# A first norm on half of its features, four projection units side by side, and a decay table that is loaded later

## The reference

```python
mod = c @ ada_w[l] + ada_b[l]
sh1, sc1, gt1, sh2, sc2, gt2 = [m[:, None, :] for m in jnp.split(mod, 6, axis=-1)]
h = rmsnorm(x, norm1_g[l]) * (1.0 + sc1) + sh1
p = h @ w_in[l]
xr, yr, q, k, v, ga, gb = jnp.split(p, cuts, axis=-1)
```

## Time and profile before

| | us |
|---|---|
| median of 3 runs | 1707.73 (1707.16 to 1708.38) |
| the profiled execution | 1710.79 |
| its span | 1709.0 |
| PE busy in it | 1653.0 |
| span until PE's first projection product | 42.56 |
| mean granted TensorE clock | 0.988 |

### The profile page before, as it was taken

One profiled execution on the slowest core, in us unless ns is written; L12 is line 12 of the kernel. 1 busy time (PEld: TensorE's weight loads), 2 busy tenths in 40 slices (PEclk: granted clock), 3 DMA queues, 4 the chain that ended last, 5 costly groups with the idle time before them and its releaser, 6 DMA issues.

```text
span 1709.0 us, 19726 instructions
## 1 busy us (share of the span) xinstructions
PE 1653.0 (97%) x7340; PEld 1345.3 (79%) x7340; DVE 982.8 (58%) x1170; ACT 801.3 (47%) x1005; POOL 785.1 (46%) x577
## 2 busy tenths in 40 slices
PE   3999999999989999999999999999999999999997
PEld 2778787877768888888887888777878888888885
DVE  6676788777637817715643767566436554155541
ACT  2565565666434425414442233676653544244442
POOL 1244443444455545554563544455573252543425
PEclk7999999999989999999999999999999999999999
DMA  9333333232222232232322322211222131321312
GB/s 367 123 123 124 123 111 124 94 128 87 85 94 98 95 101 89 99 123 99 99 86 68 111 95 71 72 42 56 75 86 76 50 109 50 99 99 50 99 50 74
DMA packets 46463, 166.89 MB, mean 98 GB/s; under 512 B 5153, under 2 KB 5281, under 8 KB 45857
## 3 DMA queue, kind: packets, MB, share of 16 engines
q1 hardware_dynamic: 46368, 165.63, 28.7%
HBM read 163.52 MB, written 2.10 MB: 97 GB/s over the span
## 4 chain that ended last, share of the span: by engine, by line
PE 89%; DVE 4%; POOL 3%; issue 1%; ACT 1%; DMA 1%; SPq 0%; POOLq 0%; DVEq 0%; ACTq 0%
PE lin L651 16%; PE lin L653 16%; PE lin L652 16%; PE big L651 7%; PE big L653 7%; PE big L652 7%; DVE scr L1580 1%; POOL sq_sum L595 1%; PE big L757 1%; PE m_o L777 1%; PE big L768 1%; PE big L770 1%; PE big L1065 1%; PE big L1063 1%; PE big L1064 1%
## 5 line engine op out<-in xcount | busy, mean ns | idle before, releaser
L617 POOL TENSOR_TENSOR w_lo<-raw,w_hi 128x512 fp32r<-128x512 f32 x200 | 283.1, 1415 | 647.4 <-ACT w_hi L1100 647.4
L651 PE MATMUL lin<-h_hi,w_hi 128*128 128x512 f32 x936 | 368.3, 394 | 4.5 <-POOL w_lo L620 1.8
L653 PE MATMUL lin<-h_hi,w_lo 128*128 128x512 f32 x936 | 364.6, 390 | 0.0
L652 PE MATMUL lin<-h_lo,w_hi 128*128 128x512 f32 x936 | 364.4, 389 | 0.0
L620 POOL TENSOR_TENSOR w_lo<-raw,w_hi 128x512 fp32r<-128x512 f32 x209 | 301.5, 1443 | 14.4 <-ACT w_hi L1100 14.4
L1100 ACT ACTIVATE w_hi<-raw 128x1024 fp32r<-128x1024 f32 (+1 forms) x209 | 217.6, 1041 | 159.8 <-PE m_b L669 50.3
L651 PEld LDWEIGHTS lin<-h_hi,w_hi 128*128 128x128 f32 x936 | 175.8, 188 | 42.4 <-issue 3.4
L653 PEld LDWEIGHTS lin<-h_hi,w_lo 128*128 128x128 f32 x936 | 175.7, 188 | 37.1
L652 PEld LDWEIGHTS lin<-h_lo,w_hi 128*128 128x128 f32 x936 | 175.9, 188 | 36.3 <-issue 0.7
L617 POOL TENSOR_TENSOR qk_hl<-raw,qk_hl 128x512 fp32r<-128x512 f32 x43 | 59.6, 1387 | 159.0 <-ACT qk_hl L1100 159.0
L651 PE MATMUL lin<-y_hi,w_hi 128*128 128x512 f32 x260 | 101.6, 391 | 0.0
(11 more groups left out here) (493 smaller groups left out, 3435.9 us busy)
## 6 DMA issues: line engine op xcount, KB each, us to landing
raw<-weights SPq DMA_DIRECT2D x245, 512.0 KB, 3.5
slab<-ada SPq DMA_DIRECT2D x32, 512.0 KB, 4.1
scr<-ada SPq DMA_DIRECT2D x16, 512.0 KB, 6.3
raw<-weights SPq DMA_DIRECT2D x10, 256.0 KB, 2.6
x<-x_t SPq DMA_DIRECT2D x2, 1024.0 KB, 6.0
out_t<-scr SPq DMA_DIRECT2D x8, 256.0 KB, 2.6
raw<-weights SPq DMA_DIRECT2D x4, 448.0 KB, 3.3
rgw<-rg_w SPq DMA_DIRECT2D x1, 1024.0 KB, 7.1
```

What stands on the lines that cost most here:

```text
L617: nc.gpsimd.tensor_tensor(lo[:, 0:4 * P], raw[:, s, 0:4 * P], hi[:, 0:4 * P].bitcast(F32), ALU.subtract).then_inc(w_half, 1)
L651: nc.tensor.matmul(psum_of(n), wh, hi(k), start=(k == 0), stop=False)
L652: nc.tensor.matmul(psum_of(n), wh, lo(k), start=False, stop=False)
L653: last = nc.tensor.matmul(psum_of(n), wl, hi(k), start=False, stop=(k == nk - 1))
```

## The change

- The slabs of the first modulation are laid out anew: slabs 0 to 7 now hold shift and scale of features 0 to 511, slabs 8 to 15 those of the other half. After 8 slabs PE forms 8 sums, and DVE, after the first 10 slabs, norms tiles 0 to 3; then come slabs 10 to 15, the second sum, tiles 4 to 7.
- The root goes to the PSUM bank `m_a` instead of `rstd`, and the scaled x of the first norm to `big[:, 2]` and `m_b` in turn instead of the four tiles `tmp`.
- PE works off tiles 0 to 3 of q0 and k0, then tiles 0 to 3 of v0 and q1, the second modulation sum, then tiles 4 to 7 of both pairs. v0 and q1 get the PSUM banks `big[:, 0]` and `big[:, 1]`; before the scores of head 0, PE waits for `v_copied` 1 and `q_copied` 2.
- A third window of two homes (in rows 2 to 5 of `y_hi` and `y_lo`) is open from q0 to v1. The homes are now q0 0, k0 1, v0 2, q1 7, k1 8, v1 0 (behind q0), xr0 1 (behind k0), yr0 2 (behind v0), ga0 0 (behind v1). Before they were q1 0 (behind q0), k1 1 (behind k0), v1 2 (behind v0), xr0 0 (behind q1), yr0 1 (behind k1), ga0 2 (behind v1).
- SP's ring: slabs 0 to 9, q0, k0, 10, 11, v0, 12 to 15, q1, 16, k1, 17, v1, 18, 19, rgw, the decay table, xr0, 20, 21, yr0, ga0, 22.
- ACT splits q0, k0, v0, then does h_hi for tiles 0 to 3, splits q1, and does tiles 4 to 7.

```diff
+NEARLY = CONST["diff"][0]
...
-            units += [("q", 0, 8), ("k", 0, 8), ("v", 0, 8), ("ada", a, 8), ("ada", a + 1, 8), ("q", 1, 8),
-                      ("ada", a + 2, 8), ("k", 1, 8), ("ada", a + 3, 8), ("v", 1, 8), ("ada", a + 4, 8)]
+            units += [("ada", i, 8) for i in range(10)] + [("q", 0, 8), ("k", 0, 8), ("ada", 10, 8), ("ada", 11, 8)]
+            units += [("v", 0, 8)] + [("ada", i, 8) for i in range(12, ADA_FIRST)]
+            units += [("q", 1, 8), ("ada", a, 8), ("k", 1, 8), ("ada", a + 1, 8), ("v", 1, 8), ("ada", a + 2, 8),
+                      ("ada", a + 3, 8)]
...
+        if h == 1:
+            units += [("ada", a, 8)]
...
-    windows = ((("w_out", 3), ("p_out", 6), None), (("a_out", 0), ("rv", 2), ("qn", HEADS - 1)))
+    windows = ((("w_out", 3), ("p_out", 6), None), (("a_out", 0), ("rv", 2), ("qn", HEADS - 1)),
+               (("q", 0), ("v", 1), None))
...
+        if (kind, j) in (("v", 0), ("q", 1)):
+            bank[n] = 2 if kind == "v" else 3
...
+        def scaled(r, k):
+            if r == 0:
+                return (big[:, 2], m_b[:])[k % 2]
+            return tmp[:, k % 4]
...
-            sp.dma_start(cst[:], consts).then_inc(cst_loaded, 16)
+            sp.dma_start(cst[:, 0:NEARLY], consts[:, 0:NEARLY]).then_inc(cst_loaded, 16)
...
                     sp.dma_start(rgw[:], rg_w).then_inc(rgw_loaded, 16)
+                    sp.dma_start(cst[:, NEARLY:NCONST], consts[:, NEARLY:NCONST]).then_inc(diff_loaded, 16)
...
-                    pair(("q", 0), ("k", 0), H, L, normed(0))
-                elif h < HEADS:
+                    for part in (range(4), range(4, DK)):
+                        if part[0]:
+                            modulation(1)
+                        pair(("q", 0), ("k", 0), H, L, normed(0), part)
+                        pair(("v", 0), ("q", 1), H, L, normed(0), part)
+                elif 1 < h < HEADS:
                     unit("q", h, H, L)
                 if h == 1:
                     unit("k", h, H, L)
+                    pe.wait_ge(v_copied, 1)
+                    pe.wait_ge(q_copied, 2)
...
-            norm_root(square_used, 8, D)
-            split_ahead(0)
-            highs(0)
+            norm_root(square_used, 8, D, m_a[:])
+            split_ahead(0, 2)
+            highs(0, range(4))
+            split_ahead(0, 3)
+            highs(0, range(4, DK))
...
-            for a in range(ADA_FIRST):
-                accumulate(a)
-            dve.wait_ge(mod_done, 2)
+            for half in range(2):
+                for a in range(10) if half == 0 else range(10, ADA_FIRST):
+                    accumulate(a)
+                dve.wait_ge(mod_done, half + 1)
...
+                if half == 0:
+                    dve.wait_ge(x_loaded, 32)
+                    dve.wait_ge(norm_rooted, 1)
+                norm_apply(0, lambda k: sm(A1 + k), lambda k: sm(MOD + k), m_a[:], 4 * half, 4 * half + 4)
...
+            dve.wait_ge(diff_loaded, 16)
             for h in range(RH):
...
-    ada = i["ada_w"][0].reshape(DK, P, 6, D).transpose(1, 2, 0, 3).reshape(P, NADA, 2, T)
+    ada = i["ada_w"][0].reshape(DK, P, 6, D).transpose(1, 2, 0, 3).reshape(P, 6, DK, 2, T)
+    ada[:, 0:2] = ada[:, 0:2].transpose(0, 3, 2, 1, 4).copy()
+    ada = ada.reshape(P, NADA, 2, T)
```

More of the change, by code:

```diff
@@ L45 @@
 _at = 0
-for _name, _n in (("ident", P), ("later_ones", 2 * P), ("ones", P), ("mask", P), ("diff", T + 3 * P),
-                  ("freq_a", 1), ("freq_r", 1)):
+for _name, _n in (("ident", P), ("later_ones", 2 * P), ("ones", P), ("mask", P), ("freq_a", 1),
+                  ("freq_r", 1), ("diff", T + 3 * P)):
     CONST[_name] = (_at, _n)
@@ L184, in bank_plan @@
             turn[ring] = 0
-        bank[n] = turn[ring] % ring
-        turn[ring] += 1
+        if (kind, j) in (("v", 0), ("q", 1)):
+            bank[n] = 2 if kind == "v" else 3
+        else:
+            bank[n] = turn[ring] % ring
+            turn[ring] += 1
         before[n] = last.get(bank[n])
@@ L511, in home @@
                 return spare[:, i - HOMES, 0], spare[:, i - HOMES, 1]
-            of = (cq_hi, cq_lo)[i - HOMES - SPARE][:].rearrange("p a t -> p (a t)")
-            return of[:, 0:8 * P], of[:, 8 * P:16 * P]
+            if i < HOMES + 2 * SPARE:
+                of = (cq_hi, cq_lo)[i - HOMES - SPARE][:].rearrange("p a t -> p (a t)")
+                return of[:, 0:8 * P], of[:, 8 * P:16 * P]
+            rows = slice(2 * (i - HOMES - 2 * SPARE) + 2, 2 * (i - HOMES - 2 * SPARE) + 4)
+            return y_hi[:, rows].rearrange("p a t -> p (a t)"), y_lo[:, rows].rearrange("p a t -> p (a t)")
         def weights_of(n):
@@ L562, in _ @@
                     sp.dma_start(inv_count, inv_counts).then_inc(inv_loaded, 16)
+                if kind == "ada" and j < ADA_FIRST:
+                    if j >= 6:
+                        sp.wait_ge(ada_used, j - 5)
+                    sp.dma_start(ada_in[:, j % 6], ada[:, j]).then_inc(ada_loaded[j % 6], 16)
+                    continue
                 if kind == "ada":
@@ L709, in modulation @@
                 for m in range(DK):
[L710 removed]
+                    at = 8 * (m // 4) + 4 * g + m % 4
+                    out = m_o[:, at:at + 1] if g < 2 else m_b[:, 8 * g - 16 + m:8 * g - 15 + m]
                     last = nc.tensor.matmul(out, acc[:, m // 4, (m % 4) * P:(m % 4 + 1) * P], c_("ones")[:, 0:1],
@@ L713, in modulation, with pair @@
                 last.then_inc(mod_done, 1)
-            def pair(a, b, hi, lo, ready):
+            def pair(a, b, hi, lo, ready, part=range(DK)):
                 na, nb = UNIT[a], UNIT[b]
                 for n in (na, nb):
-                    if BEFORE[n] is not None:
+                    if BEFORE[n] is not None and part[0] == 0:
                         pe.wait_ge(*freed(n))
-                for k in range(DK):
+                for k in part:
                     pe.wait_ge(*ready(k))
@@ L1170, in gate, with highs @@
                 act.wait_ge(rgate_done, counted(rgate_done))
-            def highs(r):
-                for k in range(DK):
+            def highs(r, part=range(DK)):
+                for k in part:
                     act.wait_ge(pre_h, DK * r + k + 1)
-                    nc.scalar.activation(h_hi[:, k], tmp[:, k % 4], ACT.Identity,
+                    nc.scalar.activation(h_hi[:, k], scaled(r, k), ACT.Identity,
                                          bias=sm(MOD + 24 * r + k)).then_inc(h_high, 1)
@@ L1595, in _, with norm_apply @@
             dve.wait_ge(dve_order, counted(dve_order))
[L1596 to L1601, removed]
+            def norm_apply(r, gain, shift, factor, first=0, last=DK):
+                for k in range(first, last + 1):
+                    if k < last:
+                        v.scalar_tensor_tensor(out=scaled(r, k), in0=x[:, k], scalar=gain(k), in1=factor,
                                                op0=M, op1=M).then_inc(pre_h, 1)
                         dve.wait_ge(pre_h, counted(pre_h))
-                    if k > 0:
+                    if k > first:
                         e = k - 1
                         dve.wait_ge(h_high, DK * r + e + 1)
-                        v.scalar_tensor_tensor(out=h_lo[:, e], in0=tmp[:, e % 4], scalar=shift(e),
+                        v.scalar_tensor_tensor(out=h_lo[:, e], in0=scaled(r, e), scalar=shift(e),
                                                in1=h_hi[:, e].bitcast(F32), op0=AD, op1=SU).then_inc(h_low, 1)
```

36 lines of the change are left out of this document (16 added, 20 removed).

## The result

The changed kernel takes 1724.72 us, the median of 4 runs (1722.45 to 1726.07), against 1707.76 for the kernel before (1707.16 to 1708.38) beside it: a ratio of 1.0094, with a 95% interval of 1.0082 to 1.0107. It is slower by 17.0 us, and the forecast was 12.8. The profiled execution took 1726.07 us with a span of 1724.0, 15.0 us more than the span of before.

What follows compares the result with a forecast made beforehand. PE, with work for 97% of the span, bounds the kernel; head 0 ends 14.7 us later, 1.9 comes back, so 1707.7 + 12.8 = 1720.5 us, range 1714 to 1725.

Steps and rivals of the forecast that it cites:

- The start: First half norm and projections: PE's first product at 31.5 us instead of 42.56, second sum ending 47.2, restart 50.4.
- The clock in the second half: PE after the second modulation sum: lower clock, q0 and k0 done at 58.5; if held, 2.2 us less, 1718.3.
- The first wait: ACT must split late-loaded xr0 before copying v0: copy at 76.8 instead of 63.16, PE idle 12 us before the transposes.
- The second wait: ACT must split yr0, landing at 87.6, before copying q1: head 0's scores at 89.3 instead of 74.62.
- only the first wait: Rival: yr0 lands before PE is through k1 (85.6), 3.7 us less, 1716.8; chance 0.05.
- The scores' clock: Variant: clock fallen also before head 0's scores, which run at half pace, 2 us more, 1722.6.
- What comes back: Between scores and suffix sums, xr0 and yr0 being split already: 1.9 us regained (1.4 to 2.4).
- The sum: Whole kernel: +14.7 for head 0's later end, -1.9 back, so +12.8 us: 1720.5.
- The mechanism: In at(), ACT splits every weight whose home is free before each copy, so copies stand behind late xr0 and yr0.
- The faster rival: No wait binds, xr0 and yr0 there in time: scores at 71.0, 5.5 us gained, 1702.2; chance 0.08.

Runs made afterwards that it cites:

- e1: Changed kernel, but ahead of copying v0 ACT splits no unit beyond v1; xr0 and yr0 are split ahead of q1's copy: 1714.82 us, ratio 1.0035.
- e2: Changed kernel, but ahead of copying v0 and q1 ACT splits nothing beyond v1; xr0 and yr0 are split ahead of k1's copy: 1706.16 us, ratio 0.9987.
- e3: Changed kernel with only SP's order altered: xr0 and yr0 loaded ahead of slab 19, gate weights and decay table ahead of slab 20: 1704.61 us, ratio 0.9980.
- e4_loads_early_busy: e3 plus 13 PE products with zeros into q0's bank, between the second modulation sum and the second half: 1708.42 us, ratio 0.9995.
- e7_busy_logs_first: e4_loads_early_busy with DVE's chain of 23 small steps (logs of decays) moved ahead of its wait for the constants: 1703.34 us, ratio 0.9973.

## Why the prediction was right, and where it was off

- **The start.** First product forecast 31.5, measured 32.07; second sum 45.3 to 47.2, measured 46.00 to 47.95; restart 50.4, measured 50.90: 0.5 to 0.8 us late throughout. Two steps inside were off without showing. The first sum took 3.15 us, not the 1.95 of before, so DVE had its first product at 27.48 instead of 25.3, but ACT was not through with v0's split before 30.45. And DVE's six accumulations took 9.70 us, not 7.9 to 8.9, so they ended at 45.75, beside PE's products and not ahead of them: the second sum waited for DVE (0.17 us), where the forecast had PE as the later one. The price of the norm's operands in PSUM, bounded at 0.75 and 1.7, was 0.76, beside POOL too.
- **The clock in the second half** was taken as low, and the window 50 to 52 has 0.50. The products of q0 and k0 were done at 59.27 against 58.5, when v0's began.
- **The first wait.** Slab 16 accumulated at 66.15 for 65.0, SP on at 66.2 for 65.1: 0.7 of this is k0's late square (63.81 for 63.1), and 0.3 the step that makes its low part, 1.45 us beside POOL (63.91) instead of 1.11. xr0 landed 8.6 us behind slab 19 (74.84), where I had 9.9 from the rows of before: the gate weights took 5.8 from issue to landing, not 7.1. The two errors cancel, 74.8 against 75.0. By the Trainium skill (DMA: Bandwidth & Descriptors, Anatomy of one DMA), whose fit is of transfers issued from GpSimd and not from SP, it was 7.9, an estimate; the measured 8.6 lies between, a little nearer to the page. v0 copied at 76.5 for 76.8; 10.42 us of idle time for 12.
- **The second wait.** Slab 18 accumulated at 82.68, forecast 82.7. yr0 landed 5.1 us after its issue, not 4.5: 88.18 for 87.6, and so the scores at 89.97 for 89.3. k1 was done at 84.6 for 85.6, so PE idled 5.32 us there and not 3.7. That yr0 landed behind k1's end also rules out the rival "only the first wait".
- **The scores' clock: the term that was mis-sized.** The forecast ran the scores at full pace, and put the lower clock before them down as a variant, 1722.6. That variant came: 4.58 us for 2.32. At k1's end the clock had been at 2.4 GHz; PE then idled 5.32 us, and the window 88 to 92 has 0.50.
- **What comes back** was put at 1.9. From the scores to the suffix sums it was 14.55 forecast, 16.40 measured; before it was 16.46. With 2.26 for the scores' clock the rest is 14.1, in the forecast's own range (14.0 to 15.1). So 2.3 came back, where 1.9 was forecast, and was lost to the clock. It came from DVE's chain, which ends with cq_lo and for which PE still waited 0.42: from its first step it took 7.7 us (98.64 to 106.32) instead of 10.0 (81.03 to 91.02), with fewer of POOL's subtractions beside it.
- **The sum.** In profiled executions +15.3 against +12.8: 0.7 from the scores' late start, 2.3 from their clock, less 0.4 from the chain behind them. The medians lie 17.0 apart, 1.7 more, since the profiled run of before was 3.0 over its median and the one of after 1.35 over its own. 1724.72 lies at the upper end of the range, 0.3 us inside it. That it is inside owes something to luck: the +2 for the scores' clock had been allowed for, but the 1.7 between the medians is no term of the forecast, and the errors of the gate weights and of slab 16 cancelled.
- **The mechanism** is shown, not only argued: e1 and e2 change what ACT does ahead of two copies, e3 what SP sends ahead of two slabs, and either makes the loss vanish. In e1, which takes only the first wait away, the second still costs.
- **The faster rival** was priced at 1702.2 and came in at 1704.6 where its condition was made true, in e3. With the logs moved as well it was 1703.2.

## What to carry to other kernels

When units get another plan of buffers, look at every place where an engine does "all that is free by now" ahead of a result that another engine waits for: a buffer that comes free earlier is there an order to wait for a load, and it needs either a load order that follows, or a limit. Before a stage is begun early, ask what the engine that ends it will run out of; here half a norm early was worth nothing without other units to fill the gap. And work that nobody waits for yet, as the chain of logs, belongs where its engine is idle, not between two steps of the critical chain.

## What was not expected of the hardware

- A vector step on 16 columns that takes 0.18 us takes 1.10 to 1.25 when it begins while POOL is in a subtraction of 128 x 512: in e4_loads_early_busy the step at 55.35 ends at 56.45, and POOL's instruction of 55.13 at 56.41; the next at 56.48 ends at 57.69, POOL's at 57.66. It looks as if the step waits for the whole POOL instruction. The norm's steps on 128 x 512 with an operand in PSUM took 0.75 to 0.76 beside POOL (32.05 in the kernel after); with both operands in SBUF they had taken 1.69. The Trainium skill (GPSIMD Engine Reference, Key points) has contention between the two for vector instructions with two SBUF inputs or in a two-port mode, which agrees in kind for the step at 55.35, with two inputs. The step at 60.91 has one and took 1.22; whether it runs in such a mode no trace here shows.
- PE's granted clock after the same instructions differed from one kernel's profile to another's: 1.00 in e4_loads_early_busy and 0.62 in e7_busy_logs_first, in the stretch from 48 to 52 us, with PE busy throughout.
